# Attention steps issued two by two on TensorE, with both biases ahead of both scores

## The chip, the cores and the metric

The kernel runs on one core of one Trainium2 chip. The metric is the device time of one execution in microseconds (us), median of several runs; lower is better. The engines that matter here are TensorE (PE, matmuls and transposes into PSUM; PEld is its weight load), ScalarE (ACT), VectorE (DVE) and the DMA queue of SyncE (SP).

## What is computed

The reference is a chain of transformer blocks on 256 tokens of width 1024 in float32: feed-forward layers, layer norms, a recurrent mixer, a gated delta rule, and attention in three places. The change touches only the attention, which is in all three places the same:

```
sc  = einsum('bnckgd,bnskd->bnkgcs', q, k) * scale  (+ a bias table)
m   = max(sc over keys)           # in one place also against a sink
pr  = exp(sc - m);  den = sum(pr) # in one place also + exp(sink - m)
o   = einsum('bnkgcs,bnskd->bnckgd', pr / den, v)
```

- "ab": 8 heads of 64 over 256 keys, with a distance bias and sinks.
- "f" and "e": 16 heads of 64 each. "f" is the context's own attention over 256 keys; "e" is the attention of the 256 tokens over 512 keys, of which the second 8 heads have a bias table.
- "m": 16 heads over 512 keys, where a score is the sum of two products (a part of its own and a shared rotated part).

## The kernel before

Every engine has a program of its own, written out in order, and the engines meet at semaphores with counts. All weights stream through a ring of 5 slots of 1 MB; ScalarE and VectorE split them into a high and a low part, and a product is three matmuls. Most of the time goes into such products. The order on each engine is the order of the Python calls; nothing plans or reorders it.

The attention is cut into steps. One step is 128 queries times 1024 scores: 4 heads of 256 keys (G = 4, in "ab" and "f") or 2 heads of 512 keys (G = 2, in "e" and "m"). `att_steps` (L1306) lists them: 4 steps for "ab", 8 of "f" followed by 16 of "e" in one run of 24, and 16 for "m". A step i goes through these stations:

1. S, scores (PE). Two PSUM banks, (0, 1) for even steps and (2, 3) for odd ones. Where there is a bias, its blocks are first written into the banks as matmuls in transpose mode (L1447, L2708; called B below), and the scores are added on top. Counted by `scored`. Needs the banks back: `exped` of step i-2.
2. M, maxima (DVE, L1359): one reduction over both banks, 1024 elements; counted by `maxed`. With sinks two small operations follow.
3. E, exponentials (ACT, L1410): G activations from PSUM to the buffer `pb[i % 3]`, each with its sum; counted by `exped`.
4. N, normalising (DVE, L1374 and L1377): a reciprocal and G multiplications in place; counted by `normed`.
5. T, transposes (PE, L1329): 8 blocks into banks 4 and 5; counted by `transposed`. Needs both banks back from the copies of the step before.
6. C, copies (ACT, L1398): banks 4 and 5 to `pt[i % 2]`, each as soon as its bank is transposed; counted by `p_copied`.
7. V, values (PE, L1344): 16 instructions into bank 6 or 7; needs C of its own step; counted by `valued`.
8. O, output (DVE, L1383): copy of V's bank; counted by `o_copied`.

`pe_attention` (L1310) issues in turn i: S(i), T(i-2), V(i-3). `dve_attention` (L1349): M(i), N(i-1), O(i-3). `act_attention` (L1388): C(i-2), E(i). Each takes a list `beside` of other work that is done in turn i: on PE before the turn (L1515, L2821, L3560), on the others at its end (L1571, L1662, L2911, L2992, L3657, L3757). That work is: in "ab" parts of the output product; in "f" the last values product and waits on values being copied out (`vB2` before turn 1); in "e" the high parts of the outputs (ACT) and their low parts (DVE), and at 17, 18 the high half and the low half of a weight slot (`slot_half`, `slot_low_half`; the low half at 18 needs the high half at 18); in "m" the last value tiles, and two weight slots (`act_m_high` in turns 2 and 6, their low halves on DVE in turns 4, 5, 9, 10).

Of the kernel before, what the change touches and what calls it, by code (L numbers as in the profile page):

```python
# [9 lines left out]
ACT = mybir.ActivationFunctionType  # L10
ALU = mybir.AluOpType
AX = mybir.AxisListType

P = 128
# [232 lines left out]
def build_program(nc, wstream, params, consts, xin, cin, pin, wab, crow, out):  # L247
    with ExitStack() as top:
# [1054 lines left out]
        def step_banks(i):  # L1303
            return (2 * (i % 2), 2 * (i % 2) + 1)
# [5 lines left out]
        def pe_attention(*parts, beside={}):  # L1310
            steps, base = att_steps(parts)
            n = len(steps)
            for i in range(n + 3):
# [7 lines left out]
                j = i - 2  # L1321
                if 0 <= j < n:
                    if j >= 1:
                        pe.wait_ge(p_copied, 2 * (base + j))
                    pe.wait_ge(normed, base + j + 1)
                    for h in range(2):
                        for k in range(4):
                            blk = 4 * h + k
                            mm = pe.transpose(ps[:, 4 + h, k * P:(k + 1) * P],  # L1329
                                              steps[j][0]["pb"][j % 3][:, blk * P:(blk + 1) * P], ident)  # L1330
                        mm.then_inc(transposed, 1)
                j = i - 3
                if 0 <= j < n:
                    A, at_j = steps[j]
                    K, per = 1024 // A["G"], A["G"] // 2
                    b = 6 + j % 2
                    if j >= 2:
                        pe.wait_ge(o_copied, base + j - 1)
                    pe.wait_ge(p_copied, 2 * (base + j + 1))
                    for hh in range(per):  # L1340
                        for k in range(K // P):
                            for g in range(2):
                                at = (g * per + hh) * K + k * P
                                mm = pe.matmul(ps[64 * g:64 * g + 64, b, hh * P:(hh + 1) * P], A["v"](at_j, hh, g, k),  # L1344
                                               A["pt"][j % 2][:, at:at + P], start=(k == 0), stop=(k == K // P - 1),
                                               skip_group_check=True)
                    mm.then_inc(valued, 1)

        def dve_attention(*parts, beside=()):  # L1349
            steps, base = att_steps(parts)  # L1350
            n = len(steps)
            for i in range(n + 3):
                if i < n:
                    A, at = steps[i]
                    G, K = A["G"], 1024 // A["G"]
                    b0 = step_banks(i)[0]
                    nm, es = (att_small[:, i % 3, 4 * m:4 * m + G] for m in (0, 3))
                    dve.wait_ge(scored, base + i + 1)
                    top_ = dve.tensor_reduce(nm, ps[:, b0:b0 + 2, :].rearrange("p b (h k) -> p (b h) k", k=K), AX.X,  # L1359
                                             ALU.max, negate=True)  # L1360
                    if A["sink"]:
                        vdone(top_)
                        vdone(dve.tensor_tensor(nm, nm, A["nsink"](at), ALU.min))
                        top_ = dve.tensor_tensor(es, nm, A["sink"](at), ALU.add)
                    top_.then_inc(maxed, 1)
                j = i - 1
                if 0 <= j < n:
                    A = steps[j][0]
                    G, K = A["G"], 1024 // A["G"]
                    den, rd, es = (att_small[:, j % 3, 4 * m:4 * m + G] for m in (1, 2, 3))  # L1370
                    dve.wait_ge(exped, base + j + 1)
                    if A["sink"]:
                        vdone(dve.tensor_tensor(den, den, es, ALU.add))
                    vdone(dve.reciprocal(rd, den))  # L1374
                    for m in range(G):
                        pm = A["pb"][j % 3][:, m * K:(m + 1) * K]
                        mul = dve.tensor_scalar(pm, pm, rd[:, m:m + 1], None, ALU.mult)  # L1377
                    mul.then_inc(normed, 1)
                j = i - 3
                if 0 <= j < n:  # L1380
                    A, at = steps[j]
                    dve.wait_ge(valued, base + j + 1)
                    dve.tensor_copy(A["o"](at), ps[:, 6 + j % 2, 0:A["G"] // 2 * P].rearrange("p (h n) -> p h n", n=P)  # L1383
                                    ).then_inc(o_copied, 1)
                if i < len(beside):
                    beside[i]()

        def act_attention(*parts, beside=()):  # L1388
            steps, base = att_steps(parts)
            n = len(steps)  # L1390
            for i in range(n + 3):
                j = i - 2
                if 0 <= j < n:
                    if j >= 2:
                        act.wait_ge(valued, base + j - 1)
                    for h in range(2):
                        act.wait_ge(transposed, 2 * (base + j) + h + 1)
                        act.activation(steps[j][0]["pt"][j % 2][:, 512 * h:512 * h + 512], ps[:, 4 + h, :],  # L1398
                                       ACT.Copy).then_inc(p_copied, 1)
                if i < n:  # L1400
                    A = steps[i][0]
                    G, K = A["G"], 1024 // A["G"]
                    banks, per = step_banks(i), G // 2
                    nm, den, es = (att_small[:, i % 3, 4 * m:4 * m + G] for m in (0, 1, 3))
                    act.wait_ge(maxed, base + i + 1)
                    if i >= 3:
                        act.wait_ge(transposed, 2 * (base + i - 2))
                        act.wait_ge(normed, base + i - 2)
                    for m in range(G):
                        e = act.activation(A["pb"][i % 3][:, m * K:(m + 1) * K],  # L1410
                                           ps[:, banks[m // per], (m % per) * K:(m % per + 1) * K], ACT.Exp,
                                           bias=nm[:, m:m + 1], accum_out=den[:, m:m + 1])
                    if A["sink"]:
                        e = act.activation(es, es, ACT.Exp)
                    e.then_inc(exped, 1)
                if i < len(beside):
                    beside[i]()
# [21 lines left out]
        def ab_scores(i, banks):  # L1439
            qt, hp = i // 2, i % 2  # L1440
# [4 lines left out]
            for g in range(2):  # L1445
                for m in range(4):
                    pe.matmul(ps[:, banks[g], m * P:(m + 1) * P], bias[:, 2 * hp + m // 2, g, m % 2, :], ident,  # L1447
                              start=(m == 0), stop=False, is_transpose=True, skip_group_check=True)
            for hh in range(2):
# [11 lines left out]
        att_ab = dict(name="ab", n=4, G=4, scores=ab_scores, pb=ab_pb, pt=ab_pt,  # L1461
# [1235 lines left out]
        def e_scores(i, banks):  # L2697
            kind, qt, h = i // 8, (i // 4) % 2, i % 4
            q_hi, q_lo = (e_qAh, e_qAl) if kind == 0 else (e_qBh, e_qBl)
            k_hi, k_lo = ((lambda r, k=k: k[r, :]) for k in (e_kAh, e_kAl)) if kind == 0 else (  # L2700
                (lambda r, k=k: k[r, h, :]) for k in (e_kBh, e_kBl))
# [3 lines left out]
            for g in range(2) if kind else ():  # L2705
                for b in range(2):
                    at = (2 * h + g) * T + b * P
                    pe.matmul(ps[:, banks[g], b * P:(b + 1) * P], slot(n)[:, at:at + P], ident, start=(b == 0), stop=False,  # L2708
                              is_transpose=True, skip_group_check=True)
            for n, (q, key) in enumerate(((q_hi, k_hi), (q_lo, k_hi), (q_hi, k_lo))):  # L2710
# [6 lines left out]
        att_e = dict(name="e", n=16, G=2, scores=e_scores, sink=None, pb=hsc_pb, pt=H_pt,  # L2717
# [719 lines left out]
        def pe_odd_mixer():  # L3437
# [122 lines left out]
            pe_attention(att_m, beside={1: lambda: pe.wait_ge(*m_a.at("v03")), 2: last_values, 3: all_copied})  # L3560
# [536 lines left out]
```

## Time and profile before

| | us |
|---|---|
| median of 3 runs | 2121.76 (2120.36 to 2122.3) |
| the profiled execution | 2119.58 |
| its span in the profile | 2118.3 |
| PE busy | 2090.3 (99%) |
| PEld busy | 1896.1 (90%) |
| DVE busy | 1495.1 (71%) |
| ACT busy | 1110.6 (52%) |
| mean granted clock of TensorE | 0.998 of full speed |

The profile is one execution, recorded per instruction, with times in microseconds from the start of the span. A busy share is an average over all stages. A timeline row gives the start, the length, the engine, the line of the kernel, the operation, output and inputs, and the number of merged instructions; in brackets stands how long the engine was idle before it and what it waited for. The three attentions lie at about 248 to 271 us ("ab"), 1238 to 1321 ("f" and "e") and 1830 to 1888 ("m").

### The profile page before, as it was taken

Reading aid. Unit: us, or ns where it says so; the run is one execution under the profiler, and the core shown is the slowest. Engines: PE = TensorE matmul, PEld = TensorE weight load, DVE = VectorE, ACT = ScalarE, POOL = GpSimd, SP = SyncE. Lnnn points to the kernel's source line nnn. Section 1 sums busy time; section 2 is a strip of 40 time slices with the busy share of each in tenths; the row PEclk is TensorE's granted clock in tenths of the full one; section 3 lists DMA queues with packets and bytes.
Section 4 is the critical chain, followed back from the end, with each engine's and each line's share of the span. In section 5 each row is a group of like instructions: output and inputs, shape, how many; then the busy total and the mean of one; then the engine's idle time right before and its main releaser. Section 6 shows DMA issues by size and latency. Waiting matters only on the chain.

```text
span 2118.3 us, 36310 instructions
## 1 busy us (share of the span) xinstructions
PE 2090.3 (99%) x15416; PEld 1896.1 (90%) x15416; DVE 1495.1 (71%) x2250; ACT 1110.6 (52%) x1749; POOL 8.6 (0%) x14
## 2 busy tenths in 40 slices
PE   9999999999999999999999999999999999999998
PEld 8999899999999899999998887988888899888997
DVE  5777877777677776667777557765555778778776
ACT  5445664446444564564447558353333467766454
POOL 0000000000000000000000000000000000000000
PEclk9999999999999999999999999999999999999999
DMA  8665445664566422256653211234444444214541
GB/s 332 245 254 206 177 176 221 239 258 161 222 253 253 166 103 99 80 229 235 242 203 131 84 60 41 100 120 159 159 159 159 177 162 159 101 41 180 198 179 60
DMA packets 51282, 359.28 MB, mean 170 GB/s; under 512 B 5680, under 2 KB 5808, under 8 KB 8496
## 3 DMA queue, kind: packets, MB, share of 16 engines
q1 hardware_dynamic: 49680, 351.30, 44.4%
q10 hardware_dynamic: 1440, 5.65, 0.7%
q8 instruction: 122, 2.00, 0.4%
q14 instruction: 40, 0.33, 0.0%
HBM read 355.88 MB, written 1.05 MB: 168 GB/s over the span
## 4 chain that ended last, share of the span: by engine, by line
PE 91%; DVE 5%; ACT 3%; issue 1%; DMA 0%; SPq 0%; ACTq 0%; DVEq 0%
PE ps L1030 9%; PE ps L1029 9%; PE ps L1028 9%; PE ps L3019 5%; PE ps L3020 5%; PE ps L3021 5%; PE ps L1112 4%; PE ps L1113 4%; PE ps L1114 4%; PE ps L461 2%; PE ps L462 2%; PE ps L463 2%; PE ps L1329 2%; PE ps L1344 2%; PE ps L2682 2%; PE ps L2684 2%
## 5 line engine op out<-in xcount | busy, mean ns | idle before, releaser
L400 DVE TENSOR_TENSOR wl<-ring,wh 128x1024 fp32r<-128x1024 f32 x380 | 453.1, 1221 | 156.3 <-ACT wh L394 156.1
L1028 PE MATMUL ps<-xs,wh 128*128 128x256 f32 x1664 | 470.9, 283 | 0.7 <-DVE wl L434 0.5
L1030 PE MATMUL ps<-xs,wh 128*128 128x256 f32 x1664 | 470.9, 283 | 0.0
L1029 PE MATMUL ps<-xs,wl 128*128 128x256 f32 x1664 | 470.8, 283 | 0.0
L394 ACT ACTIVATE wh<-ring 128x1024 fp32r<-128x1024 f32 x380 | 379.4, 1050 | 95.5 <-PE ps L1114 72.4
L1028 PEld LDWEIGHTS ps<-xs,wh 128*128 128x128 f32 x1664 | 319.0, 192 | 6.2 <-DVE wl L434 2.4
L1029 PEld LDWEIGHTS ps<-xs,wl 128*128 128x128 f32 x1664 | 319.0, 192 | 3.9
L1030 PEld LDWEIGHTS ps<-xs,wh 128*128 128x128 f32 x1664 | 319.0, 192 | 0.0
L1112 PE MATMUL ps<-wh,hh 128*128 128x512 f32 x440 | 173.0, 393 | 0.9 <-DVE hl L1227 0.9
L1113 PE MATMUL ps<-wl,hh 128*128 128x512 f32 x440 | 172.4, 392 | 0.0
L1114 PE MATMUL ps<-wh,hl 128*128 128x512 f32 x440 | 171.3, 389 | 0.0
L1153 ACT ACTIVATE sg<-ps 128x256 f32<-128x256 f32 x88 | 33.9, 385 | 216.0 <-PE ps L1030 212.7
L3019 PE MATMUL ps<-xc,fwh 128*128 128x512 f32 (+1 forms) x384 | 143.2, 373 | 1.4 <-DVE xc L759 1.2
L3020 PE MATMUL ps<-xc,fwl 128*128 128x512 f32 (+1 forms) x384 | 142.6, 371 | 0.0
L3021 PE MATMUL ps<-xc,fwh 128*128 128x512 f32 (+1 forms) x384 | 142.6, 371 | 0.0
L461 PE MATMUL ps<-xs,wh 128*128 128x256 f32 x384 | 112.3, 293 | 0.6 <-DVE wl L400 0.6
L462 PE MATMUL ps<-xs,wl 128*128 128x256 f32 x384 | 109.3, 285 | 0.0
L463 PE MATMUL ps<-xs,wh 128*128 128x256 f32 x384 | 109.3, 285 | 0.0
L400 DVE TENSOR_TENSOR fwl<-ring,fwh 128x1024 fp32r<-128x1024 f32 x77 | 92.4, 1221 | 11.6 <-ACT fwh L394 11.4
L1161 ACT ACTIVATE hh<-hT 128x256 fp32r<-128x256 f32 x110 | 46.0, 418 | 103.5 <-DVE hT L1223 92.8
L1114 PEld LDWEIGHTS ps<-wh,hl 128*128 128x128 f32 x440 | 82.6, 188 | 18.1
L1112 PEld LDWEIGHTS ps<-wh,hh 128*128 128x128 f32 x440 | 83.0, 189 | 15.6 <-issue 1.2
(576 smaller groups left out, 4468.4 us busy)
## 6 DMA issues: line engine op xcount, KB each, us to landing
ring<-wstream SPq DMA_DIRECT2D x331, 1024.0 KB, 4.9
cond_ctx<-crow ACTq DMA_DIRECT2D x3, 512.0 KB, 10.6
CN<-consts ACTq DMA_DIRECT2D x1, 1056.0 KB, 9.2
X<-xin SPq DMA_DIRECT2D x4, 256.0 KB, 5.4
ring<-wstream SPq DMA_DIRECT2D x4, 256.0 KB, 5.9
ring<-wstream SPq DMA_DIRECT2D x2, 512.0 KB, 8.3
X<-cin ACTq DMA_DIRECT2D x1, 1024.0 KB, 8.8
out<-X SPq DMA_DIRECT2D x4, 256.0 KB, 2.9
```

Of the source, the lines that this page charges most:

```text
L394: act.activation(parts_of(i)[0], gated_buffer(i) if gated(i) else tile_of(i), ACT.Copy).then_inc(high_part, tiles_done)
L400: dve.tensor_tensor(lo, w, hi.bitcast(F32), ALU.subtract).then_inc(low_part, tiles_done)
L461: pe.matmul(row(b), wh[:, w, c, :], x[:, c, 0, :], start=(c == 0), stop=False)
L1028: pe.matmul(out, wh[:, w, c, :], x_hi, start=start, stop=False, skip_group_check=True)
L1029: pe.matmul(out, wl[:, w, c, :], x_hi, start=False, stop=False, skip_group_check=True)
L1030: return pe.matmul(out, wh[:, w, c, :], x_lo, start=False, stop=True, skip_group_check=True)
L1112: pe.matmul(out, h_hi, w_hi, start=False, stop=False, skip_group_check=True)
L1113: pe.matmul(out, h_hi, w_lo, start=False, stop=False, skip_group_check=True)
L1114: mm = pe.matmul(out, h_lo, w_hi, start=False, stop=True, skip_group_check=True)
L3019: pe.matmul(out, fwh[:, w, c, :], hi, start=start, stop=False, skip_group_check=True)
L3020: pe.matmul(out, fwl[:, w, c, :], hi, start=False, stop=False, skip_group_check=True)
L3021: return pe.matmul(out, fwh[:, w, c, :], lo, start=False, stop=True, skip_group_check=True)
```

## The change

The order within the three attention functions, and nothing else of the computation, is changed. The turns now go two by two (i even):

- PE: B(i), B(i+1), S(i), S(i+1), T(i-2), V(i-3), V(i-2), T(i-1). The bias of a step is a function of its own, and each waits for the `exped` that frees its banks, so both waits stand ahead of S(i). What `beside` has for turn i+1 comes between the two biases.
- DVE: M(i), beside(i), M(i+1), N(i), O(i-3), O(i-2), N(i+1), beside(i+1).
- ACT: E(i), C(i-2), beside(i), E(i+1), C(i-1), beside(i+1).

```diff
+            for i in range(0, n + 3, 2):            # pe_attention
                 if i in beside:
                     beside[i]()
                 if i < n:
-                    if i >= 2:
-                        pe.wait_ge(exped, base + i - 1)
-                    A, at = steps[i]
-                    A["scores"](at, step_banks(i)).then_inc(scored, 1)
...
+                    biases(i)                       # waits exped >= base + i - 1 first
+                    if i + 1 in beside:
+                        beside[i + 1]()
+                    biases(i + 1)
+                    scores(i)
+                    scores(i + 1)
+                if 0 <= i - 2 < n:
+                    transposes(i - 2)
+                if i == 2 and before_values:
+                    before_values()
+                if 0 <= i - 3 < n:
+                    values(i - 3)
+                if 0 <= i - 2 < n:
+                    values(i - 2)
+                    transposes(i - 1)
...
+            for i in range(0, n + 3, 2):            # dve_attention
                 if i < n:
+                    maxima(i)
                 if i < len(beside):
                     beside[i]()
+                if i < n:
+                    maxima(i + 1)
+                    normalised(i)
+                for j in (i - 3, i - 2):
+                    if 0 <= j < n:
+                        outputs(j)
+                if i < n:
+                    normalised(i + 1)
+                if i + 1 < len(beside):
+                    beside[i + 1]()
...
+            for i in range(0, n + 3, 2):            # act_attention
+                for k in (i, i + 1):
+                    if k < n:
+                        exponentials(k)
+                    if 0 <= k - 2 < n:
+                        copies(k - 2)
+                    if k < len(beside):
+                        beside[k]()
...
-            pe_attention(att_m, beside={1: lambda: pe.wait_ge(*m_a.at("v03")), 2: last_values, 3: all_copied})
+            pe_attention(att_m, beside={1: lambda: pe.wait_ge(*m_a.at("v03")), 2: last_values},
+                         before_values=all_copied)
```

The bodies of `scores`, `transposes`, `values`, `maxima`, `normalised`, `outputs`, `copies` and `exponentials` are the old ones, with the old waits. `ab_scores` and `e_scores` are split into `ab_bias`, `e_bias` and the rest.

## Rows read from the trace of the kernel before

**Rows 1.** The chain that ended last, 1262 to 1290 us ("e"): its share by line.

```profile
by line: PE ps L1344 35.8%; PE ps L1329 33.7%; PE ps L2713 28.9%; PE ps L2708 2.1%
```

**Rows 2.** Timeline of PE, "f": scores 0; scores 2, transposes 0, scores 3.

```profile
1238.19 0.39 PE L2732 MATMUL ps<-e_kAh,e_qAh 64*128 64x256 f32 x2
...
1245.63 0.39 PE L2732 MATMUL ps<-e_kAh,e_qAh 64*128 64x256 f32 x2
...
1246.54 1.09 PE L1329 MATMUL ps<-CN,att_pb 128*128 128x128 f32 x8
1247.56 0.39 PE L2732 MATMUL ps<-e_kAh,e_qAh 64*128 64x256 f32 x2
```

**Rows 3.** Timeline of PE: bias and scores of step 22 of 24.

```profile
1308.44 0.66 PE L2708 MATMUL ps<-CN,ring 128*128 128x128 f32 x4
1309.03 0.50 PE L2713 MATMUL ps<-e_kBh,e_qBh 64*128 64x512 f32 x2
```

**Rows 4.** Timeline, "m": scores 2, scores 14, maxima 14, and the end.

```profile
1835.53 0.50 PE L3361 MATMUL ps<-m_kh,m_qh 64*128 64x512 f32 x2
...
1875.48 0.50 PE L3361 MATMUL ps<-m_kh,m_qh 64*128 64x512 f32 x2
1876.95 1.23 DVE L1359 TENSOR_REDUCE att_small<-ps 128x2 f32<-128x1024 f32 x1 [0.98 <-PE ps L3369]
...
1887.93 0.36 PE L3453 MATMUL ps<-m_yh,m_wh 128*128 128x256 f32 x1
```

**Rows 5.** Timeline of PE, end of "e": values, transposes after them, end of attention.

```profile
1316.92 1.09 PE L1344 MATMUL ps<-att_pt,e_vB 128*64 128x128 f32 x16
1317.95 1.09 PE L1329 MATMUL ps<-CN,att_pb 128*128 128x128 f32 x8
...
1320.95 0.39 PE L2682 MATMUL ps<-e_yh,e_wh 128*128 128x256 f32 x1
```

**Rows 6.** Timeline: scores of a step of "e", and its maxima.

```profile
1269.02 0.50 PE L2713 MATMUL ps<-e_kAh,e_qAh 64*128 64x512 f32 x2
1270.02 1.22 DVE L1359 TENSOR_REDUCE att_small<-ps 128x2 f32<-128x1024 f32 x1 [0.39 <-PE ps L2713]
```

**Rows 7.** Timeline: maxima of a step of "e", and the exponentials that waited for them.

```profile
1300.54 1.22 DVE L1359 TENSOR_REDUCE att_small<-ps 128x2 f32<-128x1024 f32 x1
1301.79 0.69 ACT L1410 ACTIVATE att_pb<-ps,att_small 128x512 f32<-128x512 f32 x1 [1.18 <-DVE att_small L1359]
```

**Rows 8.** Timeline of ACT, "e": first exponential of a step, and what follows both.

```profile
1268.69 0.69 ACT L1410 ACTIVATE att_pb<-ps,att_small 128x512 f32<-128x512 f32 x1
...
1270.02 0.64 ACT L2898 ACTIVATE e_yh<-e_y 128x512 fp32r<-128x512 f32 x1
```

**Rows 9.** Timeline of ACT, "m": the last copies, and the values' first weight load.

```profile
1885.48 1.09 ACT L1398 ACTIVATE att_pt<-ps 128x512 f32<-128x512 f32 x2 [0.44 <-PE ps L1329]
1886.68 0.13 PEld L1344 LDWEIGHTS ps<-att_pt,m_v 128*64 128x64 f32 x1
```

**Rows 10.** Timeline of ACT, start of "f": copies 0, exponentials 2, copies 1.

```profile
1247.23 1.09 ACT L1398 ACTIVATE att_pt<-ps 128x512 f32<-128x512 f32 x2 [0.90 <-PE ps L1329]
1248.20 0.48 ACT L1410 ACTIVATE att_pb<-ps,att_small 128x256 f32<-128x256 f32 x1
...
1250.00 1.11 ACT L1398 ACTIVATE att_pt<-ps 128x512 f32<-128x512 f32 x2
```

**Rows 11.** Timeline: three pieces of work beside the steps.

```profile
1238.30 0.60 ACT L2887 ACTIVATE e_vB<-ps 128x512 f32<-128x512 f32 x1 [4.97 <-PE ps L2814]
...
1299.40 1.23 DVE L2986 TENSOR_TENSOR ring_low<-ring,e_wh 128x1024 fp32r<-128x1024 f32 x1 [1.63 <-ACT e_wh L2905]
...
1852.69 1.93 ACT L3414 ACTIVATE m_wh<-ring 128x2048 fp32r<-128x2048 f32 x1
```

**Rows 12.** Timeline of PE, "ab": bias of step 2, and the first instruction after V(3).

```profile
254.10 1.09 PE L1447 MATMUL ps<-CN,ring 128*128 128x128 f32 x8 [1.76 <-ACT att_small L1414]
...
270.58 0.39 PE L1497 MATMUL ps<-xs,wh 128*128 128x256 f32 x1
```

More of the change, by code:

```diff
@@ L1308, in att_steps, with pe_attention, biases, scores @@
             return [(A, i) for A in parts for i in range(A["n"])], ATT0[parts[0]["name"]]
-        def pe_attention(*parts, beside={}):
+        def pe_attention(*parts, beside={}, before_values=None):
             steps, base = att_steps(parts)
             n = len(steps)
-            for i in range(n + 3):
+            def biases(i):
+                A, at = steps[i]
+                if i >= 2:
+                    pe.wait_ge(exped, base + i - 1)
+                if "bias" in A:
+                    A["bias"](at, step_banks(i))
+            def scores(i):
+                A, at = steps[i]
+                A["scores"](at, step_banks(i)).then_inc(scored, 1)
+            def transposes(j):
+                if j >= 1:
+                    pe.wait_ge(p_copied, 2 * (base + j))
+                pe.wait_ge(normed, base + j + 1)
+                for h in range(2):
+                    for k in range(4):
+                        blk = 4 * h + k
+                        mm = pe.transpose(ps[:, 4 + h, k * P:(k + 1) * P],
+                                          steps[j][0]["pb"][j % 3][:, blk * P:(blk + 1) * P], ident)
+                    mm.then_inc(transposed, 1)
+            def values(j):
+                A, at_j = steps[j]
+                K, per = 1024 // A["G"], A["G"] // 2
+                b = 6 + j % 2
+                if j >= 2:
+                    pe.wait_ge(o_copied, base + j - 1)
+                pe.wait_ge(p_copied, 2 * (base + j + 1))
+                for hh in range(per):
+                    for k in range(K // P):
+                        for g in range(2):
+                            at = (g * per + hh) * K + k * P
+                            mm = pe.matmul(ps[64 * g:64 * g + 64, b, hh * P:(hh + 1) * P], A["v"](at_j, hh, g, k),
+                                           A["pt"][j % 2][:, at:at + P], start=(k == 0), stop=(k == K // P - 1),
+                                           skip_group_check=True)
+                mm.then_inc(valued, 1)
+            for i in range(0, n + 3, 2):
                 if i in beside:
@@ new lines, in maxima @@
+            def maxima(i):
+                A, at = steps[i]
+                G, K = A["G"], 1024 // A["G"]
+                b0 = step_banks(i)[0]
+                nm, es = (att_small[:, i % 3, 4 * m:4 * m + G] for m in (0, 3))
+                dve.wait_ge(scored, base + i + 1)
+                top_ = dve.tensor_reduce(nm, ps[:, b0:b0 + 2, :].rearrange("p b (h k) -> p (b h) k", k=K), AX.X,
+                                         ALU.max, negate=True)
+                if A["sink"]:
+                    vdone(top_)
+                    vdone(dve.tensor_tensor(nm, nm, A["nsink"](at), ALU.min))
+                    top_ = dve.tensor_tensor(es, nm, A["sink"](at), ALU.add)
+                top_.then_inc(maxed, 1)
@@ new lines, in normalised @@
+            def normalised(j):
+                A = steps[j][0]
+                G, K = A["G"], 1024 // A["G"]
+                den, rd, es = (att_small[:, j % 3, 4 * m:4 * m + G] for m in (1, 2, 3))
+                dve.wait_ge(exped, base + j + 1)
+                if A["sink"]:
+                    vdone(dve.tensor_tensor(den, den, es, ALU.add))
+                vdone(dve.reciprocal(rd, den))
+                for m in range(G):
+                    pm = A["pb"][j % 3][:, m * K:(m + 1) * K]
+                    mul = dve.tensor_scalar(pm, pm, rd[:, m:m + 1], None, ALU.mult)
+                mul.then_inc(normed, 1)
@@ L1390, in act_attention @@
             n = len(steps)
[L1391 to L1417, printed above, removed]
@@ new lines, in copies, with exponentials @@
+            def copies(j):
+                if j >= 2:
+                    act.wait_ge(valued, base + j - 1)
+                for h in range(2):
+                    act.wait_ge(transposed, 2 * (base + j) + h + 1)
+                    act.activation(steps[j][0]["pt"][j % 2][:, 512 * h:512 * h + 512], ps[:, 4 + h, :],
+                                   ACT.Copy).then_inc(p_copied, 1)
+            def exponentials(i):
+                A = steps[i][0]
+                G, K = A["G"], 1024 // A["G"]
+                banks, per = step_banks(i), G // 2
+                nm, den, es = (att_small[:, i % 3, 4 * m:4 * m + G] for m in (0, 1, 3))
+                act.wait_ge(maxed, base + i + 1)
+                if i >= 3:
+                    act.wait_ge(transposed, 2 * (base + i - 2))
+                    act.wait_ge(normed, base + i - 2)
+                for m in range(G):
+                    e = act.activation(A["pb"][i % 3][:, m * K:(m + 1) * K],
+                                       ps[:, banks[m // per], (m % per) * K:(m % per + 1) * K], ACT.Exp,
+                                       bias=nm[:, m:m + 1], accum_out=den[:, m:m + 1])
+                if A["sink"]:
+                    e = act.activation(es, es, ACT.Exp)
+                e.then_inc(exped, 1)
@@ L2709, in e_scores @@
                               is_transpose=True, skip_group_check=True)
+        def e_scores(i, banks):
+            kind, qt, h = i // 8, (i // 4) % 2, i % 4
+            q_hi, q_lo = (e_qAh, e_qAl) if kind == 0 else (e_qBh, e_qBl)
+            k_hi, k_lo = ((lambda r, k=k: k[r, :]) for k in (e_kAh, e_kAl)) if kind == 0 else (
+                (lambda r, k=k: k[r, h, :]) for k in (e_kBh, e_kBl))
             for n, (q, key) in enumerate(((q_hi, k_hi), (q_lo, k_hi), (q_hi, k_lo))):
@@ L2715, in e_scores @@
             return mm
-        att_e = dict(name="e", n=16, G=2, scores=e_scores, sink=None, pb=hsc_pb, pt=H_pt,
+        att_e = dict(name="e", n=16, G=2, bias=e_bias, scores=e_scores, sink=None, pb=hsc_pb, pt=H_pt,
                      v=lambda i, hh, g, k: (e_vA[:, k, 64 * g:64 * g + 64] if i < 8 else
```

75 lines of the change are left out of this document (10 added, 65 removed).

## Prediction

> **What bounds the kernel now.** I read the table of engines first: PE is busy 99% of the span, at a mean granted clock of 0.998, so a microsecond added to or taken from PE's own line is one of the kernel's. Then the chain of waits inside the attention: it names four PE lines and no other engine [rows 1]: values, transposes, scores, biases, back to back. ACT and DVE follow a step behind and have slack. Last I read the timeline for the latency of each hand-over, because the change alters which of them lie in a row.
>
> From the scores of step 2 to those of step 22 "f" and "e" take 63.40 us [rows 2, 3], 3.17 a step; "m" takes 39.95 for 12 steps, 3.33 each [rows 4].
>
> **What the change removes.** PE loses time at each change of kind. Transposes followed by scores take 1.02 us for 8 [rows 2], values followed by transposes 1.03 for 16 [rows 5], while inside a run a transpose takes 0.117 (0.94 for 8: 1.09 busy less 0.27 for the last one, over 7) and a value 0.055 (0.87 for 16) [rows 5]. A switch is thus worth 0.1 to 0.2 us, and the first scores behind one lose another 0.1. A pair now has four switches where it had six, with a bias the two B follow transposes, the same kind. I put this at 0.35 us a pair without bias and 0.5 with, over 20 pairs 7 to 9 us: the gain, if PE stays the bound.
>
> In the Trainium skill, "TensorE: Matmul & The Clock Gate", step 1 of Part 2, says that TensorE pulls weight loads ahead of running matmuls. By that rule a switch would cost nothing and the gain would be 0; the rows above show 0.08 to 0.16 us lost at each, so the trace does not agree at changes of kind.
>
> **What it adds: a loop through three engines.** The pair on PE is S(i) S(i+1) T(i-2) V(i-3) V(i-2) T(i-1), then S(i+2). V(i-2) needs C(i-2). ACT now issues E(i) before C(i-2), and E(i) needs M(i), which needs S(i) of this same pair. So S(i) → M(i) → E(i) → C(i-2) → V(i-2) → T(i-1) → S(i+2) is closed, in order, and nothing in it can pass. Before, ACT did C(i-2) ahead of E(i), and V ran one turn later, so no such loop existed. Its length in "e":
>
> - S to M 1.00 [rows 6]; M to E 1.25 [rows 7]; both exponentials 1.33 [rows 8];
> - both copies 1.09, to the weight load of V 0.12 [rows 9];
> - V to T 1.03 [rows 5]; T to S 1.02 [rows 2].
>
> Sum 6.84 us a pair against some 5.9 now (two of S 0.9, T 1.02, V 1.02, by the spacings above). PE's own pair is about 5.5, so PE idles some 1.3 before V(i-2). In "f" four shorter exponentials take 1.80 [rows 10] in place of 1.33: 7.31. With a bias two B of 0.59 and 0.47 [rows 3] come in and T before B takes 0.94: 6.84 - 0.08 + 1.06 = 7.82. In "m" S to M is 1.47 [rows 4]: 7.31, against 6.66 now.
>
> I checked what else could be later. E(i+1) starts when C(i-2) ends, at 4.55 of the loop (copies occupy ACT 0.97 [rows 10]), and its count is up 1.33 + 0.15 (an estimate for the last sum and the semaphore, beside the 0.12 of [rows 9]) later, at 6.03, ahead of S(i+2). C(i-1), N(i), O(i-2), N(i+1) also end before they are needed.
>
> **"f" and "e".** Ten loops lead from S(2) to S(22): 3 × 7.31 + 3 × 6.84 + 4 × 7.82 = 73.7, against 63.40: +10.3.
>
> The weight slot: DVE's low half of turn 18 now stands between M(18) and M(19) and waits for ACT's high half, which runs after C(16), at 4.55 of the loop. The high half is half of a 1.93 copy [rows 11], 1.07; then 1.14 on DVE [rows 7, 11]; M(19) starts at 6.8, E(19) at 8.05, its count is up at 9.55, and B(21) and S(20) follow at 10.15 instead of 7.82: +2.3. The second half after N(19) delays M(20) by 0.5: together +2.8, as the same wait was partly there before and is inside the 63.40.
>
> Start: the wait for `vB2` was ahead of S(1) and is ahead of S(0) now; the copy ends at 1238.90 [rows 11], and S(0) ran at 1238.19 [rows 2], so with the semaphore +0.8.
>
> Tail: from S(22) to the next product 11.92 now [rows 3, 5]. Then: V(20) at 4.79, T(21) 5.82, T(22) only when C(21) has freed its banks (T to C 0.7, copies 1.09, 0.12 [rows 2, 9, 10]) 7.7, V(21) 8.8, V(22) behind C(22) 9.7, T(23) 10.7, V(23) behind C(23) 12.7, end 13.7: +1.8. In all +15.7.
>
> **"m".** Six loops from S(2) to S(14): 43.9 against 39.95: +3.9. `act_m_high` in turns 2 and 6 stands between C(i-2) and E(i+1): 1.8 on ACT [rows 11] puts the count of E(i+1) at 8.35 of the loop, and S(i+2) waits for it: 2 × 1.05 = +2.1. Start: S(2) now also waits for exped of step 1: +0.4. Tail: as above, from S(14) 14.3 against 12.45 [rows 4]: +1.9. In all +8.3.
>
> **"ab".** Two pairs only, with sinks. S(0) comes behind both biases: +1 for all that follows. PE already waited 1.76 us for E(0) before B(2) at 254.10 [rows 12]; now S(2) also waits for E(1), which has the recurrence's output and M(1) (1.1 each [rows 7, 11]) ahead of it on DVE: S(2) at about 258.7. Then one loop with the sink's small operations (about 0.5 more, an estimate), V(0) at 264.4, T(1) 265.4, 2.2 us of the output product, T(2), V(1), V(2) behind C(2) at 270.6, T(3), 1.6 us of it, V(3) done at 275.3, against 270.58 [rows 12]: +5. Bounds: +1, if DVE gets to M(1) sooner than I place it, and +7, if the clock falls in the two idle stretches of 3 and 1.7 us before S(2).
>
> **Sum.** 15.7 + 8.3 + 5 = +29.0 us. The profiled execution took 2119.58 and would take 2148.6; the median lies 2.2 above it, so 2150.8. I say 2150. Nothing after an attention gives this back, since PE runs the products behind it without a gap.
>
> **Rivals.**
> 1. *PE stays the bound.* For it: in the profile ACT and DVE are never the chain. Then V(i-2) would find C(i-2) done, and the switches' gain of 7 to 9 less about 2 for starts and tails counts: 2115, faster. It needs C(i-2) to end 1.3 us sooner than the loop has it; it decides where M to E and E together are below 1.3 us. They are 2.6 [rows 7, 8]. By the skill's rule on pulled weight loads this case would be 2122 instead.
> 2. *A shorter loop.* My hand-overs come from places where an engine stood waiting; if M or C can start on half of what it waits for, or the side work (weight slots, `vB2`, "ab") falls into waits that are there anyway, only the loops themselves stay, 14 us, less some: 2130 to 2137.
> 3. *The clock falls.* PE would idle a fifth of each loop, and in "ab" for some 3 us. Today it holds 0.998 of the full clock, through stretches that are all work. At 1.2 GHz instead of 2.4 each S, T and V in a loop takes twice its time, up to 2.9 more a pair; over all 20 loops 2205, in one of the three attentions 2160 to 2170. The table in the page has no stretch of this kind.
>
> **Chances and range.** My forecast 0.74, rival 2 0.10, rival 3 0.09, rival 1 0.05; no change, by gain and loss cancelling, 0.02. The forecast's own error is "ab" (4 below, 2 above), the weight slots (5) and 0.2 on each of 16 loops (3): 2140 to 2157. For 8 in 10 I go a little to both sides: 2136 to 2160. A measurement tells 0.2%, 4 us, from no change. Faster 0.06, within 0.03, slower 0.91.
>
> **What will show it.** PE rows of L1344 with idle before them, released by ACT L1398, about 1.2 us, once a pair: right; values with no idle before them: wrong, and rival 1. S(2) to S(22) of "f" and "e" near 76.5 us, of "m" S(2) to S(14) near 46. The chain of waits should pass through DVE L1359 and ACT L1410 and L1398. M(19) should stand far behind M(18). S(i+2) should follow T(i-1) directly except in four places. A granted clock below 1 in the three stretches is rival 3.

## The result and the profile after

The changed kernel takes 2154.36 us (median of 4 runs, 2152.53 to 2156.06) against 2121.99 of the kernel before on the same chip (2120.36 to 2122.3): ratio 1.0154, 95% interval 1.0136 to 1.0172. The prediction was 2150.0 us in a range of 2136 to 2160. Its profiled execution has a span of 2151.2 us against 2118.3, and a mean granted clock of 0.995 against 0.998.

The page of the changed kernel: the busy time of the engines, and the chain that ended last by engine.

```profile
PE 2091.6 (97%) x15416; PEld 1904.3 (89%) x15416; DVE 1497.5 (70%) x2250; ACT 1110.8 (52%) x1749; POOL 8.6 (0%) x14
...
PE 86%; ACT 6%; DVE 6%; issue 1%; DMA 0%; ACTq 0%; SPq 0%; DVEq 0%
```

PE has 1.3 us more busy time, for the same number of instructions, in a span that is 32.9 us longer. What was added is almost all idle time of PE. The list of waits, whole kernel (us in total, times, longest), names the two that grew: the first was 4.7 us in 4 waits in the kernel before, the second does not stand in its list:

```profile
ACT att_pb L1447 <- DVE att_small L1382: 34.9, 20, 2.5
...
PE ps L1347 <- ACT att_pt L1434: 21.4, 20, 2.5
```

L1347 of the changed kernel is the values V (L1344 before), L1434 the copies C, L1447 the exponentials E, L1382 the maxima M, L1332 the transposes T. The chain of waits over three loops of "e", 1275 to 1297 us, answers to [rows 1], where four PE lines stood alone; its pieces (start, length, what) of one loop stand under it:

```profile
by line: PE ps L1332 32.8%; PE ps L2763 24.7%; PE ps L1347 14.9%; ACT att_pt L1434 13.4%; ACT att_pb L1447 11.8%; issue 3.4%; ACTq L1445 0.5%
...
1282.74 1.58 PE ps L2763 x12
1284.33 1.04 PE ps L1332 x8
...
1285.39 0.04 ACTq L1445
...
1285.52 0.86 ACT att_pb L1447 x3
1286.38 0.98 ACT att_pt L1434 x2
...
1287.50 1.09 PE ps L1347 x16
```

The chain goes from scores and transposes to the exponentials and the copies on ACT, and back to the values. It enters ACT in the middle of E(i), at 1285.52, from T(i-2), which ended at 1285.37 and which C(i-2) needs. It is not what started E(i): by the timeline below E(i) started at 1284.93, 0.4 us before T(i-2) ended, released by the maxima. The loop itself, by the timeline (start, length, engine, line; in brackets the idle time before and the releaser):

```profile
1282.67 0.50 PE L2763 MATMUL ps<-e_kAh,e_qAh 64*128 64x512 f32 x2
1283.67 1.23 DVE L1382 TENSOR_REDUCE att_small<-ps 128x2 f32<-128x1024 f32 x1 [0.50 <-PE ps L2763]
1284.26 1.09 PE L1332 MATMUL ps<-CN,att_pb 128*128 128x128 f32 x8
1284.93 0.69 ACT L1447 ACTIVATE att_pb<-ps,att_small 128x512 f32<-128x512 f32 x1 [0.93 <-DVE att_small L1382]
1285.28 1.09 PE L1347 MATMUL ps<-att_pt,e_vB 128*64 128x128 f32 x16
1286.27 1.08 ACT L1434 ACTIVATE att_pt<-ps 128x512 f32<-128x512 f32 x2
1288.52 1.10 PE L1332 MATMUL ps<-CN,att_pb 128*128 128x128 f32 x8
1289.55 0.50 PE L2763 MATMUL ps<-e_kAh,e_qAh 64*128 64x512 f32 x2
```

S at 1282.67, M 1.00 later, E 1.26, C 1.34, V 1.23 (at 1287.50), T 1.02, the next S 1.03: 6.88 us. The V between, at 1285.28, is V(i-3); it has no wait. V(i-2) stood idle for 1.12. In a step of before, S and T filled the time in which M and E ran.

In "m", scores 2, the values of a plain loop, the scores behind the side work of turn 2, scores 14, and the first product behind it, where [rows 4] have 1835.53, 1875.48 and 1887.93:

```profile
1859.68 0.51 PE L3411 MATMUL ps<-m_kh,m_qh 64*128 64x512 f32 x2
...
1868.09 0.51 PE L3411 MATMUL ps<-m_kh,m_qh 64*128 64x512 f32 x2 [1.02 <-ACT att_pb L1447]
...
1880.74 1.09 PE L1347 MATMUL ps<-att_pt,m_v 128*64 128x128 f32 x16 [0.69 <-ACT att_pt L1434]
...
1905.93 0.50 PE L3411 MATMUL ps<-m_kh,m_qh 64*128 64x512 f32 x2
...
1920.15 0.39 PE L3503 MATMUL ps<-m_yh,m_wh 128*128 128x256 f32 x1
```

And "ab": biases of step 2, V(0), and the first product behind V(3), where [rows 12] have 254.10 and 270.58:

```profile
254.60 1.97 PE L1491 MATMUL ps<-CN,ring 128*128 128x128 f32 x8 [2.98 <-ACT att_small L1451]
...
265.77 1.09 PE L1347 MATMUL ps<-ab_pt,ab_v 128*64 128x128 f32 x16 [2.87 <-ACT ab_pt L1434]
...
276.30 0.39 PE L1544 MATMUL ps<-xs,wh 128*128 128x256 f32 x1
```

The eight bias transposes at 254.60 took 1.97 us, those of [rows 12] 1.09. The engine's clock had fallen from 2.4 to 1.2 GHz. Three stretches (window, its length, busy us of PE, PEld, DVE, ACT, POOL, granted clock, DMA share, GB/s) of the kernel before, the third of them behind its attention:

```profile
251.00:260.00 9.00, 6.92 (x55) 5.18 (x54) 8.46 (x24) 7.34 (x29) 0.00 (x0) 1.00 0.40 130
1254.00:1262.00 8.00, 8.00 (x99) 6.68 (x94) 7.53 (x20) 7.87 (x30) 0.00 (x0) 1.00 0.01 2
1322.00:1326.00 4.00, 4.00 (x36) 4.00 (x35) 2.77 (x2) 4.00 (x4) 0.00 (x0) 1.00 0.00 0
```

and of the changed one:

```profile
251.00:260.00 9.00, 5.32 (x26) 4.09 (x24) 6.89 (x19) 5.09 (x20) 0.00 (x0) 0.66 0.32 119
1254.00:1262.00 8.00, 5.46 (x48) 4.72 (x48) 4.52 (x13) 5.93 (x20) 0.00 (x0) 0.79 0.60 249
1322.00:1326.00 4.00, 4.00 (x21) 2.90 (x20) 3.94 (x5) 1.47 (x4) 0.00 (x0) 0.57 0.02 4
```

The first holds the wait of 2.98 us ahead of the biases, the second the start of "f", where V(0) waited 2.54 us, and the third follows a wait of 2.18 us ahead of the bias of step 21. In each PE ran part of the time at 1.2 GHz.

### The profile page after: what moved, and what is told of

It reads as the page before. It is cut to its first block, busy times and chain, and to the rows that moved or that the text cites. A ratio compares the mean times of both kernels' runs of the same rounds, so it can differ in the third digit from the quotient of the medians.

```text
span 2151.2 us, 36322 instructions
## 1 busy us (share of the span) xinstructions
PE 2091.6 (97%) x15416; PEld 1904.3 (89%) x15416; DVE 1497.5 (70%) x2250; ACT 1110.8 (52%) x1749; POOL 8.6 (0%) x14
## 3 DMA queue, kind: packets, MB, share of 16 engines
HBM read 355.88 MB, written 1.05 MB: 166 GB/s over the span
## 4 chain that ended last, share of the span: by engine, by line
PE 86%; ACT 6%; DVE 6%; issue 1%; DMA 0%; ACTq 0%; SPq 0%; DVEq 0%
PE ps L1028 9%; PE ps L1030 9%; PE ps L1029 9%; PE ps L3069 5%; PE ps L3071 5%; PE ps L3070 5%; PE ps L1112 4%; PE ps L1113 4%; PE ps L1114 4%; PE ps L461 2%; PE ps L463 2%; PE ps L462 2%; PE ps L2729 2%; PE ps L2731 2%; PE ps L2730 2%; PE ps L1960 2%
## 5 line engine op out<-in xcount | busy, mean ns | idle before, releaser
L1112 PEld LDWEIGHTS ps<-wh,hh 128*128 128x128 f32 x440 | 83.0, 189 | 15.7 <-issue 1.2
```

Of the source, the lines that this page charges most:

```text
L1112: pe.matmul(out, h_hi, w_hi, start=False, stop=False, skip_group_check=True)
```

## The experiments

Theory A is the prediction's: PE's order and ACT's order together close the loop S, M, E, C, V, T, and side work that stands inside a pair lies on it. Theory C was formed from the profile after: what the prediction missed is the clock behind the long waits. Rivals are named with each run. Each run has its own runs of the kernel before on the same chip, at 2121.37 to 2122.27 us. Where two variants are compared, they ran on different chips as a rule, so their excess over the kernel before is what is compared.

### ScalarE's copies ahead of its exponentials

```
 for k in (i, i + 1):
+    if 0 <= k - 2 < n:
+        copies(k - 2)
     if k < n:
         exponentials(k)
-    if 0 <= k - 2 < n:
-        copies(k - 2)
```

> The changed kernel, with ScalarE's order of a step turned: copies of the transposes first, exponentials second (C(i-2), E(i), C(i-1), E(i+1) in place of E(i), C(i-2), E(i+1), C(i-1)). Theory A (two orders together make the loop, that of TensorE and that of ScalarE): V(i-2) no longer waits for an exponential, but S(i+2) now waits for E(i+1), which stands behind C(i-1), which follows T(i-1). The loop in 'e' becomes S S 1.96, T 1.02, copy and hand-over 1.2, V 0.95, T 1.02, copy 1.15, E 1.33, hand-over 0.12, together 8.8 us a pair against 6.88 measured; in 'm' about 10 against 7.35, in 'f' about 9.7 against 7.4. 7 x 1.9 + 3 x 2.3 + 7 x 2.7 = 39, so about 2190 us (2180 to 2205). Rival (what costs is only that E is issued ahead of C): the wait is gone and TensorE's own work bounds the pair again, 2115 to 2125 us.

Measured: 2186.21 us, ratio 1.0306 (1.0290 to 1.0321). Two loops of "e", the first scores of each:

```profile
1288.27 0.51 PE L2763 MATMUL ps<-e_kAh,e_qAh 64*128 64x512 f32 x2 [2.23 <-ACT att_pb L1447]
...
1297.65 0.51 PE L2763 MATMUL ps<-e_kAh,e_qAh 64*128 64x512 f32 x2 [2.23 <-ACT att_pb L1447]
...
1305.59 0.51 PE L2763 MATMUL ps<-e_kAh,e_qAh 64*128 64x512 f32 x2 [2.23 <-ACT att_pb L1447]
```

The wait of the values shrank or went, and 2.23 us stand ahead of the scores instead. The first of these loops takes 9.38 us, at a granted clock of 0.82 (8 transposes 1.97 us at 1290.06), the second 7.94 at 1.00. At the full clock the loop is thus 1.06 longer than the 6.88 of the changed kernel, and 0.9 shorter than the 8.8 expected. The clock fell again and again in this run (mean 0.985 against 0.995), and that made up for the difference: that 2186 lies so near the expected 2190 is partly luck. Theory A holds in kind and the rival falls: ACT's order alone is not the cause, it is what the order leaves between T(i-1) and the next scores.

### The side work behind the pair

```
-18: lambda: slot_low_half(0), 19: lambda: slot_low_half(1),
+19: lambda: (slot_low_half(0), slot_low_half(1)),
...
-beside=[idle, last_values] + [lambda: act_m_high(8)] + [idle] * 3 + [lambda: act_m_high(9)] + [idle] * 9
+beside=[idle, last_values] + [idle, lambda: act_m_high(8)] + [idle] * 3 + [lambda: act_m_high(9)] + [idle] * 8
```

> The changed kernel, with the side work that stands inside a pair moved behind it: VectorE's two half slots of turns 18 and 19 both behind N(19), ScalarE's high parts of turns 2 and 6 of 'm' behind the second step (turns 3 and 7). Theory A (work beside the steps is on the loop when it stands between the two of a pair): the loop of S18 to S20 goes from 10.14 to about 7.3 us (-2.8), and the two loops of 'm' of 8.4 us to about 7.4 (-1.0 each), together -4.9, so about 2149.5 us. Rival (it stood beside TensorE's work, or what follows waits for it in its new place): no change, 2154 us.

Measured: 2152.88 us, ratio 1.0146 (1.0131 to 1.0162), 1.5 below the changed kernel where 4.9 were expected; by the medians alone that is not told from no change. The profile tells two answers apart. In "m", from S(0) to the end of attention, it is 63.94 us against 66.12: -2.2, as expected, and no scores wait there any more. In "e" the loop from S(18) fell from 10.14 to 7.75, and the next rose from 8.36 to 10.88:

```profile
1320.24 2.35 DVE L3036 TENSOR_TENSOR ring_low<-ring,e_wh 128x1024 fp32r<-128x1024 f32 x2
1322.51 2.34 DVE L1382 TENSOR_REDUCE att_small<-ps 128x2 f32<-128x1024 f32 x2
1323.76 0.69 ACT L1447 ACTIVATE att_pb<-ps,att_small 128x512 f32<-128x512 f32 x1 [3.58 <-DVE att_small L1382]
1326.32 1.71 PE L1347 MATMUL ps<-att_pt,e_vB 128*64 128x128 f32 x16 [2.63 <-ACT att_pt L1434]
```

The two half slots now follow N(19) and end at 1322.51, so M(20) starts 2.5 us after its scores did (1319.98) instead of 1.0, E(20) and C(18) after it, and V(18) waits 2.63, behind which the clock falls too. A loop through DVE has no place at which 2.3 us of work on DVE are free; the rival was right for this half.

### Half of every copy on VectorE

```
 act.wait_ge(transposed, 2 * (base + j) + 1)
 act.activation(pt[:, 0:512], ps[:, 4, :], ACT.Copy).then_inc(p_copied, 1)
...
+def second_half(j):            # behind maxima(i + 1) for i - 2, behind normalised(i + 1) for i - 1
...
+    dve.wait_ge(transposed, 2 * (base + j) + 2)
+    dve.tensor_copy(pt[:, 512:1024], ps[:, 5, :]).then_inc(p_copied, 1)
```

> The changed kernel, with the second half of every copy of the transposes on VectorE (C(i-2)'s behind M(i+1), C(i-1)'s behind N(i+1)) in place of ScalarE. Theory A (the loop is S, M, E, C, V, T): V(i-2) then waits for half of C on ScalarE, 0.55 us in place of 1.09, and the half on VectorE is done by then (M(i+1) ends 2.5 us after S(i) does). The loop shortens by 0.45 to 0.5 us in the 18 pairs that it bounds, -8 to -9 us, so about 2145.5 us. Rival (M(i+1) delays the half copy, or N(i) is late behind it): no change or slower, 2154 to 2160 us.

Measured: 2157.64 us, ratio 1.0173 (1.0158 to 1.0189): no gain. The loop of "e" is 6.75 us against 6.88, with another releaser:

```profile
1290.95 0.68 DVE L1414 COPY att_pt<-ps 128x512 f32<-128x512 f32 x1
...
1291.78 1.09 PE L1347 MATMUL ps<-att_pt,e_vA 128*64 128x128 f32 x16 [1.00 <-DVE att_pt L1414]
```

DVE was busy without a gap there (its low part of y stands between M(i) and M(i+1)), so its half came as late as ACT's whole one. From B(0) of "ab" to V(3) done it took 33.0 us against 28.6. The run is no test of the length of C, but it shows the rival's mechanism: M(i+1) and the side work delay the half copy. The 8 to 9 us expected did not come.

### Half of C(i-2) alone, in "m" alone

The same edit, for even steps of "m" only.

> The changed kernel, with the second half of C(i-2) alone, and in 'm' alone, on VectorE behind M(i+1); C(i-1) and the other attentions stay as they are. With all copies halved VectorE was full in 'ab', 'f' and 'e'; in 'm' it has 5.8 us of work in a pair of 7.35. Theory A: the idle time of V(i-2) in 'm' (0.67 to 0.69 us) falls by about 0.5 and each of the 7 loops to about 6.9 us, together -3.3 us, 2151 us. Rival (the half on VectorE comes as late as the whole one on ScalarE, or another chain of 7.35 us takes over, E(i+1) for S(i+2)): 2154 us.

Measured: 2152.16 us, ratio 1.0139 (1.0126 to 1.0153), 29.9 above its kernel before in place of 32.4; the intervals overlap, and the rows below give 1.2. Scores to scores the six loops from S(2) take 7.93, 7.74, 7.95, 6.85, 7.75 and 6.86 us. In the two of 6.85 the wait of the values is gone but for 0.20; in the two of 7.75 the half on DVE ended last; the two of 7.9 hold side work of ACT. A wait for DVE's half, and one in a loop of 6.85:

```profile
1874.64 1.09 PE L1347 MATMUL ps<-att_pt,m_v 128*64 128x128 f32 x16 [1.09 <-DVE att_pt L1414]
...
1889.44 1.09 PE L1347 MATMUL ps<-att_pt,m_v 128*64 128x128 f32 x16 [0.20 <-ACT att_pt L1443]
```

Where only C is shorter the loop is shorter by 0.5, the time taken off C: it is a term of the loop. Where DVE's half is late, 0.4 is lost instead, which is why the run gains less than the 3.3 expected: S(2) to S(14) takes 45.08 in place of 46.25.

### Dummy transposes in the long waits

```
 def biases(i):
+    if i == 2 and A["name"] == "ab": fill(6, 20)      # 20 transposes of ident into bank 6
+    if i == 21: pe.wait_ge(o_copied, base + 17); fill(6, 12)
...
 def values(j):
+    if j == 0 and A["name"] in ("ab", "f"): fill(b, 16)
```

> The changed kernel, with dummy transposes of the identity into an unused bank in four waits of TensorE: 20 ahead of the bias of the third step of 'ab', 16 ahead of V(0) of 'ab' and of 'f', 12 ahead of the bias of step 21. They add no useful work. Theory C (what the prediction missed, 3 to 4 us, is the clock that falls behind these waits): the granted clock stays at 1.00 at 253 to 260, 1257 to 1260 and 1322 to 1325 us, and the time falls by 3 to 6 us, to about 2150 us. Rival (the falls have another cause, or the work at half clock stood beside other work): the clock falls all the same or the time stays, 2154 us or up to 2 us more.

Measured: 2151.87 us, ratio 1.0143 (1.0126 to 1.0160). The same three stretches:

```profile
251.00:260.00 9.00, 6.79 (x58) 5.64 (x56) 7.02 (x19) 5.09 (x20) 0.00 (x0) 1.00 0.43 148
1254.00:1262.00 8.00, 7.20 (x85) 6.36 (x82) 6.03 (x14) 5.77 (x20) 0.00 (x0) 1.00 0.71 262
1322.00:1326.00 4.00, 4.00 (x42) 3.08 (x40) 3.25 (x3) 1.24 (x3) 0.00 (x0) 1.00 0.00 0
```

The clock stayed at 2.4 GHz in all three, with work that computes nothing. From B(0) of "ab" to V(3) done it took 26.98 us against 28.58 (-1.6), and the first loop of "f" 7.31 against 8.85 (-1.5). The fill of step 21 cost 0.6 net: it had to wait for a free bank and came late. Together -2.5, by medians as by stages, in place of the 3 to 6 expected; the intervals of the two kernels overlap, so the verdict rests on the stages. Theory C holds for these two places. In every other profiled run with "ab" two by two the granted clock of 250 to 262 us was 0.72 to 0.78.

For step 21 it does not hold. The profile of the next run, "ab" one by one, has the same wait there, and the clock did not fall (granted 1.00 from 1316.20 to 1324.50). Its biases 21, scores 20 and scores 22:

```profile
1315.63 0.66 PE L2799 MATMUL ps<-CN,ring 128*128 128x128 f32 x4 [2.17 <-ACT att_pb L1491]
1316.22 0.50 PE L2810 MATMUL ps<-e_kBh,e_qBh 64*128 64x512 f32 x2
...
1324.49 0.50 PE L2810 MATMUL ps<-e_kBh,e_qBh 64*128 64x512 f32 x2
```

The loop takes 8.27 us at the full clock, and 8.27 again in the run on half of C in "m"; in the changed kernel, at the low one, it takes 8.36. The fall cost 0.1 there. The other 0.5 above 7.75 is the second half slot on DVE, which ends after the scores do and delays M(20), as the prediction had it.

### Each attention back by itself

In both runs one attention is issued in the order of the kernel before, on all three engines (one step, one transposes, one values).

> The changed kernel with 'ab' alone back in the order of the kernel before on all three engines; 'f', 'e' and 'm' stay two by two. Theory A (the attentions cost independently of one another: 'ab' 5.7 us by the two profiles, 'f' and 'e' 17.5, 'm' 9.0): about 2148.7 us, that is 26.7 above the kernel before. Rival (what 'ab' ends later is caught up where the next section waits for its weights): 2154 us, no change.

Measured: 2148.09 us, ratio 1.0120 (1.0107 to 1.0134), 25.9 above its kernel before in place of 32.4: "ab" costs 6.5 us.

> The changed kernel with 'm' alone back in the order of the kernel before on all three engines; 'ab', 'f' and 'e' stay two by two. Theory A (the shares add up: 'ab' 6.3 us by its own run, 'm' 9.0 by the two profiles, 'f' and 'e' the rest, 17): 2154.4 - 9.0 = 2145.4 us. Rival ('m' is followed by the output products, whose weights bound the end anyway): 2150 us or more.

Measured: 2144.10 us, ratio 1.0108 (1.0092 to 1.0123), 22.7 above its kernel before: "m" costs 9.6 us. The interval of each ratio is 3 to 4 us to either side, so these shares are rough; the rows (5.7 and 9.0) agree with them. The rest of the 32.4, 16.2, falls to "f" and "e" by subtraction; no run has these alone, so that the shares add up is not tested. Both rivals fall, which had the later sections give the loss back (2154, and 2150 or more).

### The exponentials of both steps together

Here the order of TensorE is kept and that of ScalarE and VectorE follows it, in "m" alone:

```
 PE    S(i) S(i+1) T(i-2) V(i-3) V(i-2) T(i-1)    S(i) waits for E(i-2), S(i+1) for E(i-1)
-ACT   E(i)   C(i-2) E(i+1) C(i-1)
+ACT   C(i-2) E(i)   E(i+1) C(i-1)
-DVE   M(i) M(i+1) N(i)   O(i-3) O(i-2) N(i+1)
+DVE   M(i) N(i-1) M(i+1) O(i-3) N(i)   O(i-2)
```

> 'ab', 'f' and 'e' in the order of the kernel before; 'm' two by two on TensorE as in the changed kernel, but S(i) waits for E(i-2) alone and only S(i+1) for E(i-1), ScalarE runs C(i-2), E(i), E(i+1), C(i-1), and VectorE M(i), N(i-1), M(i+1), O(i-3), N(i), O(i-2). Theory A (a pair costs more only because ScalarE put E(i) ahead of C(i-2)): V(i-2) has its copies 1.2 us after T(i-2), behind V(i-3), and the exponentials are done by T(i-1); TensorE's own rows of a pair (S S 2.49, T and V 4.08) are the bound, 6.6 us against 6.66 before: 2120 to 2122 us, at best 1 to 2 us below the kernel before. Rival (two by two costs in any order, since V(i-2) follows T(i-2) too closely): V(i-2) still waits 0.5 us or more in a pair, 2125 to 2128 us.

Measured: 2123.28 us against 2122.22, ratio 1.0001 (0.9992 to 1.0010). One pair of PE's timeline, scores to scores, with no wait in it:

```profile
1857.39 0.51 PE L3458 MATMUL ps<-m_kh,m_qh 64*128 64x512 f32 x2
...
1859.93 1.09 PE L1337 MATMUL ps<-CN,att_pb 128*128 128x128 f32 x8
...
1862.93 1.09 PE L1337 MATMUL ps<-CN,att_pb 128*128 128x128 f32 x8
1863.95 0.51 PE L3458 MATMUL ps<-m_kh,m_qh 64*128 64x512 f32 x2
```

6.56 us, against 7.35 of the changed kernel and 6.80 of the kernel before. This is the sharpest test of theory A: inside the pairs the same order on TensorE costs nothing once C(i-2) is not behind E(i) and the scores do not wait for both exponentials. The rival falls. The run changes ACT's order, DVE's order and the wait of the scores together; which of them would do alone is not shown. It also measures the gain of fewer changes of kind by itself: 0.24 us a pair. From S(0) to the end of attention it is still 59.02 against 57.86: V(0) waited 0.83 in the pair of step 2, and the end behind step 14 took 14.31 instead of 12.45. So the time is 1.1 above its kernel before, not the 0 to 2 below it that were expected.

> As the run before it, and 'e' in the same order too (VectorE's two half slots at turns 20 and 22). Theory A: a pair of 'e' without bias 5.7 us (S S 1.6, T and V 4.1) against 5.88, one with bias 6.65 (B 0.95 for both) against 7.06; 3 x 0.2 + 4 x 0.4 = 2.2 us below the run before it, so about 2119 us, 3 us below the kernel before. Rival (V(i-2) or S(i+1) waits for ScalarE): 2122 to 2130 us.

Measured: 2126.22 us, ratio 1.0019 (1.0011 to 1.0028), slower than the run before it. A pair without bias took 5.62 and 5.87 us, but with both biases ahead B(i+1) waited 0.36 to 0.89 for its exponential, and at the end of "e" T(22) stood 2.79. The rival was right here.

> The kernel before, with the pairs of steps 4 to 13 of 'm' alone in the order of the run 'm_exponentials_together'; the first two pairs and the last two, with what follows them, stay one by one. That run took 32.76 us for these five pairs against 34.10 of the kernel before (6.55 against 6.80 a pair), lost 0.6 in the pair of step 2 (V(0) waited 0.83) and 1.9 behind step 14. Theory A: the five pairs alone give -1.3 us, 2121 us. Rival (the loss at the end follows from the order of the last full pair and stays): 2122 to 2123 us.

Measured: 2121.63 us, ratio 1.0000 (0.9992 to 1.0009). Four pairs took 6.52 each, the first 8.16: S(5) waited 1.36 us for E(3), behind 1.9 us of side work on ACT. The pairs gave 1.1 and the entry took 1.4, so neither case of the expectation was right: the loss stood at the start of the stretch, not at its end.

> As the run before it, and the pairs of turns 10 to 17 (steps 2 to 9 of 'e') in the same order, where each step's bias stands ahead of its own scores and waits for its own exponential. In the run 'e_and_m_exponentials_together' a pair without bias took 5.62 us at best against 5.88, and the losses stood at the first pair, at the pairs with both biases ahead, at the half slots and at the end, which all stay out here. Theory A: 4 x 0.25 = 1.0 us below the run before it, about 2120 us, 2.3 us (0.1%) below the kernel before. Rival (VectorE, with its low parts of y in these pairs, is full at 5.9 us): no gain, 2121 us.

Measured: 2121.54 us, ratio 1.0000 (0.9991 to 1.0009). From S(2) of "f" to the end of "e" 75.10 us against 75.32 before: -0.2, not -1.0.

> As the run 'e_and_m_together_but_ends', with the high part of turn 2 of 'm' on ScalarE one turn later, behind E(3). In that run S(5) waited 1.36 us for E(3), since the high part of 1.9 us stood ahead of E(3) and two by two asks for E(3) one T and one V sooner; it took back what the five pairs gave. Theory A: the wait goes, from S(4) to S(14) of 'm' 32.9 us in place of 34.2, the time 1.3 us lower, 2120 us, below the kernel before by 1 to 1.5 us in its rows, which the median can hardly tell. Rival (C(2) and E(4) come late behind the moved part, and the wait moves to V(2) or S(6)): 2121.5 us.

Measured: 2119.63 us against 2122.27, ratio 0.9988 (0.9979 to 0.9997). The wait is gone:

```profile
1843.83 0.50 PE L3458 MATMUL ps<-m_kh,m_qh 64*128 64x512 f32 x2
1845.09 0.39 PE L3458 MATMUL ps<-m_kh,m_qh 64*128 64x512 f32 x2
...
1876.45 0.50 PE L3458 MATMUL ps<-m_kh,m_qh 64*128 64x512 f32 x2
```

S(4) to S(14) takes 32.62 us against 34.10 of the kernel before. This version is faster than the kernel before by 2.6 us in the medians (0.6 to 4.5 by the interval); its rows explain 1.5 in "m" and 0.2 in "e", the rest is not shown to be its doing.

## Why the prediction was right, step by step

| term | predicted | in the profile after | by its own run |
|---|---|---|---|
| loop of "e", of "f", with bias, of "m" | 6.84, 7.31, 7.82, 7.31 | 6.88, 7.38, 7.75, 7.35 | |
| S(18) to S(20), with the weight slot | 10.15 | 10.14 | |
| S(22) to the end of "e"; S(14) to that of "m" | 13.7; 14.3 | 13.78; 14.22 | |
| "f" and "e" | +15.7 | +17.5 | +16.2 (the rest) |
| "m" | +8.3 | +9.0 | +9.6 |
| "ab" | +5 | +5.7 | +6.5 |
| sum | +29.0 | +32.9 (0.7 outside) | +32.4 |

**The loop** was right in place and length, within 0.1 us a pair, and the idle time ahead of V(i-2) was 1.12 in "e" where I had said about 1.2. It could be summed from six hand-overs of the kernel before, although no loop existed there, because those between engines were taken from rows where the receiving engine stood waiting [rows 6, 7] or from a copy's end to the weight load [rows 9]. S(2) to S(22) took 78.27 us where I expected 76.5, and "m" S(2) to S(14) 46.25 where I expected 46.0.

**The gain of fewer changes of kind** I put at 0.35 us a pair for rival 1; the runs that let it show give 0.24 to 0.28. In the changed kernel it lies inside PE's idle time and is worth nothing.

**Side work inside a pair** (+2.8 and 2 × 1.05) came out as worked out: the two loops with the weight slot took 10.14 and 8.36 us, 3.0 above twice 7.75, and 1.02 stood twice ahead of the scores. S(i+2) followed T(i-1) directly except there and in "ab", four places. That it could be moved away freely would have been wrong for the weight slot.

**What was missed** is 4.4 us of median, 3.9 of the profiled execution. By place it is 1.8 in "f" and "e", 0.7 in "m", 0.7 in "ab" and 0.7 behind "m". The mis-sized terms are the first pairs: I let V(0) of "f" and the stretches of "ab" run at the full clock and kept its fall as a bound of "ab" and as rival 3. By the run with dummy transposes it cost 1.5 in the first loop of "f" (8.85 for 7.31), nearly all of the 1.8. In "ab" it cost 1.6 where only 0.7 are missing: my working of "ab" without it was 0.9 too long, and the two errors partly cancel. In "m", S(0) stood 0.64 us for the copy `v03`, which had been asked for one step later; I had not seen this wait. Behind step 21 the clock fell too, but cost 0.1: the scores of two steps took 2.79 us instead of 1.59, and the wait for the copies behind them was 0.20 in place of the 1.64 of the run at the full clock. Rival 3 thus held in part: in these places, not in the plain loops, which kept the full clock with PE idle for 1.12 of every 6.88 us in "e" and 1.6 of every 7.38 in "f". The same columns as above, for the plain loops of "f" and "e" in the changed kernel:

```profile
1262.00:1320.00 58.00, 47.39 (x513) 38.09 (x510) 41.78 (x86) 42.27 (x113) 0.00 (x0) 1.00 0.05 19
```

The Trainium skill, "TensorE: Matmul & The Clock Gate", Part 1, has the array's clock halved after too little activity; the trace agrees, with transposes at 1.97 us for eight in place of 1.09 behind a wait of 2.98.

The length of one wait does not decide it here. A wait of 3.04 us near 1918 us of the kernel before, for a residual that has nothing to do with the change, left the clock at 1.00; the same wait of the changed kernel was followed by a fall:

```profile
1918.33 0.36 PE L1064 MATMUL ps<-xs,wh 128*128 128x256 f32 x1 [3.04 <-ACT xs L859]
...
1950.86 0.55 PE L1064 MATMUL ps<-xs,wh 128*128 128x256 f32 x1 [3.04 <-ACT xs L859]
```

And the wait of 1.76 us in "ab" in its old order was followed by a fall in three of the seven profiled runs that have it.

**One reading to mend.** I wrote that the chain of waits should pass through DVE's maxima. It does not: it goes back from C(i-2) to T(i-2), which C(i-2) needs and which had ended 0.9 us before C(i-2) could start, and passes over what started E(i). The timeline's bracket and the list of waits name the maxima.

What stays open: the 0.7 us behind "m". The fall near 1950 us stands there; at its place the next products came 1.3 us later, some of which the following stretch took back. It stands in the profile after and in some of the others, not in that of before, and I did not test it. So a difference of about 1 us between two profiled executions proves nothing by itself.

## What to carry to other kernels

When steps are grouped on one engine, write out the cycle (here S, M, E, C, V, T and the next S) that each consumer now closes through the other engines, and read its length from rows in which the receiver stood waiting; if it exceeds the bounding engine's own work, the orders of the other engines must be changed with it. Group the exponentials when the scores are grouped, and look at the first and last pair and at all side work: here they took back more than fewer changes of kind gave. This kernel keeps its bounding engine at 99% and had little to win from its order: 0.1% in the best version found.

## What the runs showed of the hardware

A change of kind on TensorE between scores, transposes and values costs: four changes in place of six gave 0.24 to 0.28 us a pair in "m". Idle stretches of 1.1 us in every 6.9 left the granted clock at 1.00 for tens of microseconds. Single waits of 2.2 to 3.0 us were followed in the changed kernel by stretches at 0.57 to 0.79, but not always: 2.17 us in another run and 3.04 in the kernel before were not, and 1.76 was in three runs of seven. With 20 and 16 dummy transposes inside two of the waits it stayed at 1.00. While the clock was low, 8 transposes took 1.97 us and 16 values 1.97 us against 1.09; the loop paid for that only where no wait stood behind them (1.5 us in "f", 0.1 at step 21).
